# Layer norm over feature tiles: sums of tile pairs in column tiles, statistics on quarters of the tokens, late conditioning chunks moved

## The reference

```python
mod = einsum('bd,de->be', silu(c), w_ada[l]) + b_ada[l]      # 6 x 1024 columns: shift, scale, gate, twice
h = x * (1 + sc1) + sh1
y, s_new, vn = token_mixer(h, ...)                            # w_in, gated mixing and recurrence, w_out
x = layer_norm(ALPHA * x + gt1 * y, ln1_w[l], ln1_b[l])
h = x * (1 + sc2) + sh2
f = swiglu(h, ...) if l % 2 == 0 else moe_swiglu(h, ...)      # dense, or top 2 of 8 experts
x = layer_norm(ALPHA * x + gt2 * f, ln2_w[l], ln2_b[l])

def layer_norm(x, w, b):
    mu = mean(x); var = mean((x - mu) ** 2)
    return (x - mu) * rsqrt(var + 1e-5) * w + b
```

## Time and profile before

| | |
|---|---|
| time, median of 3 runs | 1574.04 us (1573.84 to 1576.1) |
| profiled execution, span from first to last instruction | 1570.6 us |
| TensorE busy | 1495.2 us, 95% |
| VectorE busy | 1173.1 us, 75% |
| ScalarE busy | 907.7 us, 58% |
| GpSimd busy | 62.4 us, 4% |
| mean granted TensorE clock | 0.981 |

### The profile page before, as it was taken

The page is one execution under the profiler, slowest core; times in us unless marked ns, Lnnn a source line. Parts: engine busy times, 40 slices in busy tenths (PEclk is TensorE's granted clock), DMA queues, the critical chain, the costliest instruction groups (busy, mean ns, idle before and its releaser), DMA issues.

```text
span 1570.6 us, 22379 instructions
## 1 busy us (share of the span) xinstructions
PE 1495.2 (95%) x8616; PEld 1260.9 (80%) x8616; DVE 1173.1 (75%) x1261; ACT 907.7 (58%) x845; POOL 62.4 (4%) x92
## 2 busy tenths in 40 slices
PE   5899999999999899997999999999999999999995
PEld 1668876999999699885788888888878888888874
DVE  2444677655557666766988989889898898888987
ACT  2445544433333566444777677676777766767772
POOL 3000001000000200002000000000000000000000
PEclk8899999999999999998999999999999999999998
DMA  9997536644444743240999999999999999999994
GB/s 331 345 370 261 181 102 206 208 161 161 140 156 132 253 146 108 64 128 17 333 355 355 338 338 363 334 355 339 344 347 334 352 345 336 357 345 367 349 372 169
DMA packets 217742, 416.06 MB, mean 265 GB/s; under 512 B 7923, under 2 KB 79773, under 8 KB 217638
## 3 DMA queue, kind: packets, MB, share of 16 engines
q1 hardware_dynamic: 214086, 402.31, 73.5%
q0 software_dynamic: 3552, 12.33, 2.6%
HBM read 407.79 MB, written 6.82 MB: 264 GB/s over the span
## 4 chain that ended last, share of the span: by engine, by line
PE 54%; DVE 4%; issue 1%; ACT 1%; DMA 0%; DVEq 0%; ACTq 0%
PE bank L680 15%; PE bank L682 15%; PE bank L681 15%; PE bank L1087 1%; PE bank L1125 1%; PE bank L683 1%; PE bank L685 1%; PE bank L684 1%; DVE w_lo L1625 1%; PE bank L784 1%; PE bank L1168 1%; PE bank L1169 1%; PE bank L1038 0%; DMA raw_ring<-in_e_gate_dram 0%; DVE xT L1728 0%
## 5 line engine op out<-in xcount | busy, mean ns | idle before, releaser
L1625 DVE TENSOR_TENSOR w_lo<-raw_ring,w_hi 128x2048 fp32r<-128x2048 f32 x264 | 604.4, 2291 | 96.9 <-ACT w_hi L1340 96.1
L1340 ACT ACTIVATE w_hi<-raw_ring 128x2048 fp32r<-128x2048 f32 x264 | 506.7, 1920 | 230.1 <-PE bank L682 224.6
L680 PE MATMUL bank<-w_hi,xg_hi 128*128 128x512 f32 (+1 forms) x768 | 293.3, 382 | 2.2 <-DVE xg_lo L2139 1.4
L682 PE MATMUL bank<-w_hi,xg_lo 128*128 128x512 f32 (+1 forms) x768 | 288.9, 376 | 0.0
L681 PE MATMUL bank<-w_lo,xg_hi 128*128 128x512 f32 (+1 forms) x768 | 288.8, 376 | 0.0
L683 PE MATMUL bank<-act_hi,w_hi 128*128 128x320 f32 x736 | 232.9, 316 | 12.7 <-DVE act_lo L1675 9.1
L684 PE MATMUL bank<-act_lo,w_hi 128*128 128x320 f32 x736 | 228.1, 310 | 0.0
L685 PE MATMUL bank<-act_hi,w_lo 128*128 128x320 f32 x736 | 228.0, 310 | 0.0
L1616 DVE TENSOR_TENSOR w_lo<-raw_ring,w_hi 128x2048 fp32r<-128x2048 f32 x65 | 148.7, 2288 | 80.5 <-ACT w_hi L1267 80.3
L682 PEld LDWEIGHTS bank<-w_hi,xg_lo 128*128 128x128 f32 x768 | 144.3, 188 | 29.2
L680 PEld LDWEIGHTS bank<-w_hi,xg_hi 128*128 128x128 f32 x768 | 144.4, 188 | 27.9 <-DVE xg_lo L2139 1.6
(11 more groups left out here) (332 smaller groups left out, 1896.0 us busy)
## 6 DMA issues: line engine op xcount, KB each, us to landing
raw_ring<-in_e_gate_dram SPq DMA_DIRECT2D x90, 1024.0 KB, 5.1
raw_ring<-in_e_up_dram SPq DMA_DIRECT2D x90, 1024.0 KB, 5.2
raw_ring<-in_e_down_dram SPq DMA_DIRECT2D x88, 1024.0 KB, 5.0
raw_ring<-in_w_ada_dram SPq DMA_DIRECT2D x30, 1024.0 KB, 6.7
raw_ring<-in_w_in_dram SPq DMA_DIRECT2D x24, 1024.0 KB, 9.7
raw_ring<-in_w_ff_gate_dram SPq DMA_DIRECT2D x11, 1024.0 KB, 5.2
raw_ring<-in_w_ff_up_dram SPq DMA_DIRECT2D x11, 1024.0 KB, 5.2
raw_ring<-in_w_ff_down_dram SPq DMA_DIRECT2D x11, 1024.0 KB, 4.8
```

The lines of the kernel that those rows point to most:

```text
L680: pe.matmul(out, xh, wh, start=start, stop=False)
L682: return pe.matmul(out, xl, wh, start=False, stop=stop)
L1340: act.activation(w_hi[:, (NSPLIT + i) % SPL, :], raw[:, s, :], ACT.Copy).then_inc(hi_ready.sem, 1)
L1625: dve.tensor_tensor(w_lo[:, r, :], raw[:, s, :], w_hi[:, r, :].bitcast(F32), ALU.subtract).then_inc(lo_ready.sem, 1)
```

## The change

A norm's sums are taken for two tiles at once: four matmuls, two tiles and two squares, each with 32 columns of ones in a column tile of its own, so that bank rows 0 to 63 hold the sums of two half sets and rows 64 to 127 those of the squares. ScalarE copies that bank; eight small matmuls (`statistics`) add the halves and lay quarter j of the tokens (80 of them) on partitions 32j to 32j + 31; square, variance, root and reciprocal run on 80 columns; one full matmul gives the mean on all partitions and four (`spread_root`) give the inverse root back, which ScalarE copies from four banks. In the output projection VectorE's `center` of the tile before stands ahead of the wait for the next projection.

Of the six late conditioning chunks in norm (0, 0), four stay ahead of the ladder (one ahead of `spread_root`, three behind it) and two go into it behind kk == 3. In norm (0, 1) three stay ahead and three go into `win_first(1)` behind kk == 2, 3 and 4. The transposes stand at kk == 5, at kk == 7 and behind the ladder. ScalarE's row copies all stand behind `modulated`.

```diff
-        bank = [ctx.enter_context(nc.psum_tensor(f"bank{i}", [P, 512], F32)) for i in range(8)]
+        banks = ctx.enter_context(nc.psum_tensor("bank", [P, 8, 512], F32))
+        bank = [banks[:, i, :] for i in range(8)]
...
-        sum_mm = signal("sum_mm", 2)
-        md_ready = signal("md_ready", 2)
+        stat_mm = signal("stat_mm", 2 * 3)
+        stat_act = signal("stat_act", 2 * 5)
+        stat_dve = signal("stat_dve", 2 * 2)
         less_mean = signal("less_mean", 2 * 3)
-        msq_ready = signal("msq_ready", 2)
-        var_ready = signal("var_ready", 2)
-        sd_ready = signal("sd_ready", 2)
...
+        TQ = T // 4
+        LN_SUM = 1.0 / (32.0 * D)
+        QUARTER_SUMS, MEAN_SUMS, ROOT_ROWS = range(3)
+        SUMS_COPIED, MEAN_SQUARED, ROOTED, MEAN_COPIED, ROOT_COPIED = range(5)
+        VARIANCE, INVERSE = range(2)
...
-                pool.wait_ge(md_ready.sem, md_ready.at(l, i))
+                pool.wait_ge(stat_act.sem, stat_act.at(l, 5 * i + MEAN_COPIED))
                 pool.wait_ge(sq_ready.sem, sq_ready.at(l, KD * i + KD - 1))
                 pool.wait_ge(dev_ready.sem, dev_ready.at(l, KD * i + KD - 1))
-                pool.wait_ge(sum_mm.sem, sum_mm.at(l, i))
+                pool.wait_ge(sq_used.sem, sq_used.at(l, KD * i + KD - 1))
...
-                if half == 0 and p == NEARLY // 2 + 1:
-                    pe.wait_ge(var_ready.sem, var_ready.at(0, 0))
...
-                if half == 0 and p - adas[0] == 1:
+                if turn and half == 0 and p - adas[0] == 1:
...
+                    if l and kk in (2, 3, 4):
+                        ada(NALL - 5 + kk, turn=False)
+                    if l and kk in (5, 7):
+                        ada_turn()
...
-            def sums(l, i, m):
-
-                a, b = sum_banks(i)
+            def pair_sums(l, i, m):
+
+                a = sum_banks(i)[0]
                 if m == 0:
                     pe.wait_ge(sh_ready.sem, sh_ready.at(l, i))
-                pe.wait_ge(dev_ready.sem, dev_ready.at(l, KD * i + m))
-                last = pe.matmul(a[:, 0:T], ones[:], xT[:, m, :], start=(m == 0), stop=(m == KD - 1))
-                if m == KD - 1:
-                    last.then_inc(sum_mm.sem, 1)
-                pe.wait_ge(sq_ready.sem, sq_ready.at(l, KD * i + m))
-                pe.matmul(b[:, 0:T], ones[:], lnx[:, m % 2, :], start=(m == 0), stop=(m == KD - 1)).then_inc(sq_used.sem, 1)
+                pe.wait_ge(dev_ready.sem, dev_ready.at(l, KD * i + m + 1))
+                pe.wait_ge(sq_ready.sem, sq_ready.at(l, KD * i + m + 1))
+                first, end = m == 0, m == KD - 2
+                for j in range(2):
+                    pe.matmul(a[32 * j:32 * j + 32, 0:T], ones[:, 0:32], xT[:, m + j, :], start=first, stop=end)
+                for j in range(2):
+                    last = pe.matmul(a[64 + 32 * j:96 + 32 * j, 0:T], ones[:, 0:32], lnx[:, j, :], start=first, stop=end)
+                    last.then_inc(sq_used.sem, 1)
+
+            def statistics(l, i):
+
+                a, b = sum_banks(i)
+                pe.wait_ge(stat_act.sem, stat_act.at(l, 5 * i + SUMS_COPIED))
+                for c, rs in ((a, slice(0, 64)), (b, slice(64, 128))):
+                    for j in range(4):
+                        last = pe.matmul(c[32 * j:32 * j + 32, 0:TQ], ones[rs, 0:32], lnx[rs, 0, TQ * j:TQ * (j + 1)],
+                                         start=True, stop=True)
+                last.then_inc(stat_mm.sem, 1)
+                pe.matmul(bank[3][:, 0:T], ones[0:64, :], lnx[0:64, 0, :], start=True, stop=True).then_inc(stat_mm.sem, 1)
+
+            def spread_root(l, i):
+
+                pe.wait_ge(stat_act.sem, stat_act.at(l, 5 * i + MEAN_COPIED))
+                pe.wait_ge(stat_dve.sem, stat_dve.at(l, 2 * i + INVERSE))
+                for j in range(4):
+                    js = slice(32 * j, 32 * j + 32)
+                    last = pe.matmul(bank[1 + j][:, 512 - TQ:512], ones[js, :], nmean[js, 0:TQ],
+                                     start=True, stop=True)
+                last.then_inc(stat_mm.sem, 1)
...
-                    sums(l, 0, j - 2)
+                    if j % 2:
+                        pair_sums(l, 0, j - 3)
...
-                sums(l, 0, KD - 2)
-                sums(l, 0, KD - 1)
+                pair_sums(l, 0, KD - 2)
+                statistics(l, 0)
                 if l == 0:
-                    for i in range(NEARLY, NEARLY + LATE):
-                        ada(i)
+                    ada(NEARLY, turn=False)
+                spread_root(l, 0)
+                if l == 0:
+                    for i in range(NEARLY + 1, NEARLY + 4):
+                        ada(i, turn=False)
...
+                        if kk == 3:
+                            ada(NEARLY + 4, turn=False)
+                            ada(NEARLY + 5, turn=False)
+                        if kk in (5, 7):
+                            ada_turn()
...
-                                if c == NFC - 1 and m >= 4:
-                                    sums(l, 1, m - 4)
+                                if c == NFC - 1 and m == 6:
+                                    pair_sums(l, 1, 0)
...
-                    for m in range(KD - 4, KD):
-                        sums(l, 1, m)
-                    for i in range(NEARLY + LATE, NALL):
-                        ada(i)
+                    for m in range(2, KD, 2):
+                        pair_sums(l, 1, m)
+                    statistics(l, 1)
+                    ada(NEARLY + LATE, turn=False)
+                    spread_root(l, 1)
+                    for i in range(NEARLY + LATE + 1, NALL - 3):
+                        ada(i, turn=False)
...
-                act.wait_ge(sum_mm.sem, sum_mm.at(l, i))
-                a = sum_banks(i)[0][:, 0:T]
-                act.activation(lnx[:, 3, :], a, ACT.Copy, scale=1.0 / D).then_inc(md_ready.sem, 1)
-                act.activation(lnx[:, 2, :], a, ACT.Square, scale=1.0 / D).then_inc(msq_ready.sem, 1)
-                act.wait_ge(var_ready.sem, var_ready.at(l, i))
-                act.activation(nmean[:], nmean[:], ACT.Sqrt, bias=eps[:, 0:1]).then_inc(sd_ready.sem, 1)
+                a = sum_banks(i)[0]
+                act.wait_ge(sq_used.sem, sq_used.at(l, KD * i + KD - 1))
+                act.activation(lnx[:, 0, :], a[:, 0:T], ACT.Copy).then_inc(stat_act.sem, 1)
+                act.wait_ge(stat_mm.sem, stat_mm.at(l, 3 * i + QUARTER_SUMS))
+                act.activation(lnx[:, 2, 0:TQ], a[:, 0:TQ], ACT.Square, scale=LN_SUM).then_inc(stat_act.sem, 1)
+                act.wait_ge(stat_dve.sem, stat_dve.at(l, 2 * i + VARIANCE))
+                act.activation(nmean[:, 0:TQ], nmean[:, 0:TQ], ACT.Sqrt, scale=32.0 * 32.0, bias=eps[:, 2:3]).then_inc(stat_act.sem, 1)
+                act.wait_ge(stat_mm.sem, stat_mm.at(l, 3 * i + MEAN_SUMS))
+                act.activation(lnx[:, 3, :], bank[3][:, 0:T], ACT.Copy, scale=LN_SUM).then_inc(stat_act.sem, 1)
+                act.wait_ge(stat_mm.sem, stat_mm.at(l, 3 * i + ROOT_ROWS))
+                act.activation(nmean.rearrange("p (j t) -> p j t", j=4), banks[:, 1:5, 512 - TQ:512], ACT.Copy).then_inc(stat_act.sem, 1)
...
-                    ada_rows(NALL - 2)
-                    ada_rows(NALL - 1)
+                    for i in range(NEARLY + LATE, NALL):
+                        ada_rows(i)
...
-                if l == 0:
-                    for i in range(NEARLY, NEARLY + 4):
-                        ada_rows(i)
                 modulated(l, 1, hf)
                 if l == 0:
-                    for i in range(NEARLY + 4, NEARLY + LATE):
+                    for i in range(NEARLY, NEARLY + LATE):
                         ada_rows(i)
...
-                    for i in range(NEARLY + LATE, NALL - 2):
-                        ada_rows(i)
...
-                dve.wait_ge(msq_ready.sem, msq_ready.at(l, i))
-                dve.wait_ge(sq_used.sem, sq_used.at(l, KD * i + KD - 1))
-                dve.scalar_tensor_tensor(nmean[:], sum_banks(i)[1][:, 0:T], 1.0 / D, lnx[:, 2, :], ALU.mult,
-                                         ALU.subtract).then_inc(var_ready.sem, 1)
+                dve.wait_ge(stat_act.sem, stat_act.at(l, 5 * i + MEAN_SQUARED))
+                dve.wait_ge(stat_mm.sem, stat_mm.at(l, 3 * i + QUARTER_SUMS))
+                dve.scalar_tensor_tensor(nmean[:, 0:TQ], sum_banks(i)[1][:, 0:TQ], LN_SUM, lnx[:, 2, 0:TQ], ALU.mult,
+                                         ALU.subtract).then_inc(stat_dve.sem, 1)
+                dve.wait_ge(stat_act.sem, stat_act.at(l, 5 * i + ROOTED))
+                dve.reciprocal(nmean[:, 0:TQ], nmean[:, 0:TQ]).then_inc(stat_dve.sem, 1)
+                dve.wait_ge(stat_act.sem, stat_act.at(l, 5 * i + MEAN_COPIED))
                 minus_mean(l, i, 0)
-                dve.wait_ge(sd_ready.sem, sd_ready.at(l, i))
-                link(dve.reciprocal(nmean[:], nmean[:]))
+                dve.wait_ge(stat_act.sem, stat_act.at(l, 5 * i + ROOT_COPIED))
...
```

(6 more changed lines are left out.)

5 lines of the change are left out of this document (3 added, 2 removed).

## The result

The changed kernel ran in 1586.13 us (median of 4, 1583.72 to 1587.3), the kernel before beside it in 1575.07 (1573.84 to 1577.51): ratio 1.0063 [1.0042, 1.0085], slower by 9.9 us (the recorded ratio of the runs; the two medians as they stand are 11.1 us apart). A second set of runs gave 1.0067 [1.0045, 1.0090]. The forecast was +4.85 us, 1578.9, with its own range from 1576 to 1582.5: slower, as forecast, and by more than forecast. The profiled execution took 1585.3 us, its instructions 1583.5, 12.9 more than the 1570.6 of before.

A forecast was written before the change was run, and what follows sets the result against it. TensorE, 95% busy, was taken as the bound nearly everywhere, so its own time and its waits at each norm count. Terms -8.9 + 0.1 - 2.0 - 0.8 + 5.05 + 5.4 + 6.0 = +4.85 on 1574.04: 1578.9 us, range 1576 to 1582.5.

The forecast's parts named there:

- Step 1: Output projections: sums by pairs in column tiles, 0.68 us a pair, save 4.45 us per layer, -8.9 us.
- Step 4: Behind the ladders: ScalarE's late row copies hold the next weights and reads, +5.05 us in layer 0, +5.4 in layer 1.
- Steps 2 and 3: Norm's chain 0.8 us shorter; ladder behind it +0.1 us in layer 0, -2.0 in layer 1; last norm -0.8.
- step 3: Ladder behind the norm: in layer 0 starts 2.2 us earlier but holds more, +0.1 us; in layer 1 -2.0 us.
- Step 5: TensorE's clock falls in the new waits behind the ladders, 3.4 us, and ahead of them, 1.3 each: +6.0 us.
- The rivals in which the clock holds: TensorE's clock holds in the new waits: 1572.9 us, chance 0.16; with layer 1's end recovered too, 1568.6, chance 0.10.
- the one in which it comes back at the router: Clock recovers at layer 1's router and gather matmuls, -4.3 us, while the other falls stand: 1574.6 us, chance 0.12.
- the one in which the column tiles don't overlap: Pair sums' column tiles run unshared, 1.58 us more on each pair in the loops, +11.4 us: 1590.3 us, chance 0.04.

The follow-up runs named there:

- the kernel with early turns: Changed kernel with the next weights' w_hi copy behind the first row copy and transposes at kk 4, 5 and 6, none behind the ladder: ratio 1.0012.
- the norm part alone: Kernel before with only pair sums, statistics on quarters and earlier centring; chunks, transposes and row copies as before: ratio 0.9964, run again 0.9952.
- the best built on it: Norm part alone with each set's last chunk in the ladder, mean's matmul first, GpSimd subtracting from the last pair of tiles only: ratio 0.9949.

## Why the prediction was right in kind and short in size

The time was forecast at 1578.9 us and came at 1586.1; the direction and the largest term were right, the sum was 5 to 8 us short.

**Step 1** (sums in the projections, -4.45 a layer) held: 0.68 us a pair, -4.0 and -4.2. The centring did cost nothing: inside the loops TensorE waits for no pair.

**Step 4** (ScalarE held, +5.05 and +5.4) held to 0.2 us: +5.2 and +5.4, with the waits forecast (3.54 for `w_lo`, 5.43 for the reads), and the kernel with early turns took them away.

**Steps 2 and 3 failed**, by 5.6 us, of which some 4.3 are the overlap of GpSimd and VectorE and 1.3 the clock. "The first low part ... comes at +12.3" and "so it starts at +12.35: 2.2 us earlier": the low part came at +14.3 and the ladder at +14.4; in layer 1 the ladder was 2.0 us later than forecast, at the router the norm 1.5 us. In the first two the clock had fallen inside the statistics, which moved the ladder by 0.6 to 0.7 us each (12.28 us behind the last pair of sums with the fall, 11.62 without it). The multiply's start was itself forecast well: +7.6 predicted, +7.6 in layer 1 of the changed kernel (726.17 less 718.60) and in layer 0 of the norm part alone; +8.5 in the changed kernel's layer 0, where the clock fell inside the statistics. The rest is behind it. I had seen that "GpSimd starts its subtractions later and overlaps VectorE longer", and gave it the price of the one overlapped multiply in the trace, 1.37 us, of which only the first 0.7 us met GpSimd (270.56; GpSimd's last subtraction ended at 271.24). In full overlap the multiply is 1.8 to 2.05 us and the 128-column modulation, priced at nothing, 1.5 us for 0.29. The changed kernel with GpSimd left only the last pair shows it: 1.6, 1.9 and 1.2 us sooner at the three places, the clock's part taken off. Its ratio shows only part, so for that much of the miss the mechanism is shown in the trace and its worth in time stays between 2.4 and 6 us.

The other half of step 3, the ladder's contents, was right in layer 0, +2.5 for +2.3. In layer 1 it was +5.3: 1.3 of clock (ten matmuls at 0.27 us apart instead of 0.15) and 4.0 for the 3.3 forecast. The wait ahead of the router, which the forecast shortened to 3.2 us, was 5.1.

**Step 5** (clock, +6.0) was right in sum and partly in place: 1.9 us behind layer 0's ladder and 1.4 behind layer 1's (3.4 forecast), 1.3 in the first matmuls of layer 1's ladder, and in place of a fall at layer 0's ladder two falls in the statistics, 0.6 to 0.7 us each at the ladders (the 1.3 us above): 5.9. That the sum fits so well is luck, since two of its places weren't forecast. The rivals in which the clock holds are out; so is the one in which it comes back at the router (0.54 in the windows there, 0.56 before), and the one in which the column tiles don't overlap (0.68 us a pair). The clock is the term that moves: two executions of one program had it at different places and the same end.

**What is left**: the expert stage's 2.8 us in the profiled execution, 1.3 us behind layer 1's ladder that no step had, 1.8 us of remainders (0.7 in step 1, 0.9 in the ladders' contents, 0.2 in step 4), and on the other side the 1.9 us by which the changed kernel came sooner to its first output projection. The ratios, 9.9 and 10.6 us, lie 2 to 3 us below the profile.

No version that computes the whole norm beat the norm part alone by more than the measurement tells: 0.9952 to 0.9964 for it, 0.9949 for the best built on it. It is the version to keep; it beats the kernel before by 6 to 8 us and the changed one by some 17.

## What to carry to other kernels

When two engines' work is moved so that it newly overlaps, don't price the overlap by an instruction that met it only in part: look which of the pair's instructions is in flight during which, and take the row with full overlap or bound it by the other engine's whole instruction plus its own. When work is moved behind a loop to shorten what stands ahead, ask first what the loop's start waits for; here TensorE idled 2.7 and 3.4 us in front of the ladders once the chunks were gone, so taking them away saved 0.8 and 1.4 us there and cost 2.5 and 4.0 inside. And an in-order engine that gets the last of three dependent copies behind a loop holds everything queued behind it until the loop's end, whatever that is.
